# A layer whose expert weights stream through a ring of SBUF slots: 12 slots in place of 9, paid for by moving the front buffers into the late slots

## The reference

```python
def moe_ffn(x2, w_router, b_router, w_gu, b_gu, w_down, b_down):
    logits = (x2 @ w_router + b_router).astype(jnp.float32)
    top_vals, top_idx = lax.top_k(logits, TOP_K)                  # 4 of 32
    gates = jax.nn.softmax(top_vals, axis=-1).astype(x2.dtype)
...
        h = x2[tok] @ w_gu[e] + b_gu[e]                           # 1024 x 2048 for each expert
        g = jnp.minimum(h[:, :D_FF], SWIGLU_LIMIT)
        u = jnp.clip(h[:, D_FF:], -SWIGLU_LIMIT, SWIGLU_LIMIT)
        y = (u + 1.0) * (g * jax.nn.sigmoid(SWIGLU_ALPHA * g))
        return y @ w_down[e] + b_down[e]                          # 1024 x 1024 for each expert
```

## Time and profile before

| | |
|---|---|
| median of 3 runs | 1331.33 us (1329.54 to 1331.73) |
| profiled execution, device time | 1332.64 us |
| its span, first to last instruction | 1330.8 us |
| PE busy | 1113.0 us, 84% |
| DVE, ACT, POOL busy | 359.2, 157.1, 24.3 us |
| read from HBM | 443.69 MB, 334 GB/s over the span |
| mean granted TensorE clock | 0.939 |

### The profile page before, as it was taken

One profiled execution on the slowest core, in us unless ns is written; L12 is line 12 of the kernel. 1 busy time (PEld: TensorE's weight loads), 2 busy tenths in 40 slices (PEclk: granted clock), 3 DMA queues, 4 the chain that ended last, 5 costly groups with the idle time before them and its releaser, 6 DMA issues.

```text
span 1330.8 us, 19889 instructions
## 1 busy us (share of the span) xinstructions
PE 1113.0 (84%) x7904; PEld 463.9 (35%) x7905; DVE 359.2 (27%) x1183; ACT 157.1 (12%) x360; POOL 24.3 (2%) x26
## 2 busy tenths in 40 slices
PE   4999999999998665768956799797986987989895
PEld 3758845845332111112311133232321322323231
DVE  1513521124232121112211133231222322323224
ACT  0020300211111000001100011110110110111111
POOL 6000000000000000000000000000000000000000
PEclk9999999996999888789988799998998997999998
DMA  9933346305999999999899957999899899897980
GB/s 313 318 123 131 131 168 269 127 12 221 413 419 427 426 428 425 426 427 385 360 427 425 426 253 322 426 426 425 335 426 426 331 427 426 334 429 330 427 374 32
DMA packets 57460, 445.04 MB, mean 334 GB/s; under 512 B 4784, under 2 KB 7872, under 8 KB 24192
## 3 DMA queue, kind: packets, MB, share of 16 engines
q1 hardware_dynamic: 55888, 438.35, 79.9%
q0 software_dynamic: 976, 5.26, 1.2%
q10 hardware_dynamic: 576, 1.14, 0.3%
HBM read 443.69 MB, written 1.05 MB: 334 GB/s over the span
## 4 chain that ended last, share of the span: by engine, by line
PE 53%; DMA 41%; DVE 3%; SPq 2%; issue 1%; ACT 0%; DVEq 0%
DMA ring<-in_w_down 32%; PE bank L728 16%; PE bank L759 8%; DMA ring<-in_w_gu 8%; PE bank L425 6%; PE bank L440 6%; PE bank L685 4%; PE bank L616 2%; PE bank L672 2%; SPq L319 2%; DMA ring<-in_xT 1%; PE bank L678 1%; PE bank L738 1%; PE bank L723 1%; PE bank L604 1%
## 5 line engine op out<-in xcount | busy, mean ns | idle before, releaser
L728 PE MATMUL bank<-ring,memT_sb 128*32 128x512 f32 x3264 | 418.9, 658 | 138.9 <-DMA ring<-in_w_gu 138.9
L728 PEld LDWEIGHTS bank<-ring,memT_sb 128*32 128x32 f32 x3264 | 105.0, 116 | 423.9 <-issue 211.9
L1249 DVE TENSOR_SCALAR memK<-bank 128x256 f32<-128x256 f32 x51 | 21.7, 425 | 660.8 <-PE bank L728 660.8
L759 PE MATMUL bank<-ring,memV 128*32 128x512 f32 x1632 | 196.1, 598 | 0.2 <-DMA ring<-in_w_down 0.2
L685 PE MATMUL bank<-memV,memK 64*128 64x512 f32 x416 | 106.1, 629 | 0.7 <-ACT memV L921 0.7
L913 ACT ACTIVATE memK<-memK 128x256 f32<-128x256 f32 x51 | 21.2, 417 | 554.6 <-DVE memK L1249 554.6
L759 PEld LDWEIGHTS bank<-ring,memV 128*32 128x32 f32 x1632 | 47.9, 109 | 76.5 <-issue 61.1
L425 PE MATMUL bank<-ring 128*128 128x256 f32 x320 | 72.6, 390 | 0.8 <-issue 0.8
L425 PEld LDWEIGHTS bank<-ring 128*128 128x128 f32 x320 | 62.4, 196 | 9.9 <-issue 1.0
L685 PEld LDWEIGHTS bank<-memV,memK 64*128 64x128 f32 x416 | 37.2, 193 | 78.3 <-issue 76.7
L672 PE MATMUL bank<-res,memT_sb 128*32 128x256 f32 x832 | 56.5, 390 | 0.0
(11 more groups left out here) (250 smaller groups left out, 753.2 us busy)
## 6 DMA issues: line engine op xcount, KB each, us to landing
ring<-in_w_gu SPq DMA_DIRECT2D x128, 2048.0 KB, 31.9
ring<-in_w_down SPq DMA_DIRECT2D x64, 2048.0 KB, 27.0
ring<-in_w_in SPq DMA_DIRECT2D x5, 2048.0 KB, 21.1
ring<-in_w_ck SPq DMA_DIRECT2D x2, 2048.0 KB, 12.3
ring<-in_w_out SPq DMA_DIRECT2D x2, 2048.0 KB, 7.9
ring<-in_w_cv SPq DMA_DIRECT2D x2, 2048.0 KB, 8.2
ring<-in_w_cq SPq DMA_DIRECT2D x2, 2048.0 KB, 8.5
ring<-in_w_co SPq DMA_DIRECT2D x2, 2048.0 KB, 7.9
```

Source lines behind the costliest of these rows:

```text
L728: ins = mm(hidden(g), xg[:, kk, c, :], gate_and_up(w[:, kk, :], g), start=False, stop=2 * c + kk == KT - 1, skip_group_check=True)
L759: ins = mm(strip(7, 2 * d + b), actT[:, b, 2 * c + gg, :], wd[:, gg, b, 512 * d:512 * d + 512], start=c == 0 and gg == 0, stop=c == 1 and ...
```

## The change

- `RING` is 12 and `UNROLL` is 2. The ring then holds two experts. It is 192 KB of each partition.
- Slots 8 to 11 exist in full, and in the front they hold what had buffers of their own: `memV` and `ebuf` in slot 8, `memK` and `memT_sb` in slot 9, `qbuf` and the tables (`early_c`) in slot 10, `xk`/`tT` and `lnp` in slot 11; `akT` and `akrot` lie in slot 7. The small buffers of the experts' passes are in one tensor `wk`.
- The first twelve pieces wait: slots 6 and 7 for `mixer_done`; 4, 5, 0, 1 for their front pieces; slot 10 for the last score matmul of the cross-attention (`cs_ready`, L587 before), slot 9 for its last transpose (`cpT_ready`, L594), slot 8 for unit `oT1` (L604), slots 2 and 3 for `co_t1` (L616), slot 11 for unit `logit` (L633).
- POOL issues no load. ACT issues its loads at the start behind the tables, the first layer norm's parameters and `b_down` with them. The second norm's parameters are issued by ACT when the first norm is done. The third's are issued by SP into slot 6 when the last pass of expert 30 has used its first piece.
- The values are computed once for each row (two groups of eight matmuls in place of four), and ACT copies them to the four windows in five copies in place of one. The 64 columns of zeros are gone.
- `mark_gates` multiplies in place (`eq` for `gq`) and waits for `hot_ready`; `act` is written over `ucl`. The memset of `ysb` stands behind the router's last reduction, and that of `scatT` behind `sums_open`.

```diff
-UNROLL = 3
+UNROLL = 2
-RING = 9
+RING = 12
-RING_ORDER = [6, 7, 4, 5, 0, 1, 2, 3, 8]
+RING_ORDER = [6, 7, 4, 5, 0, 1, 10, 9, 8, 2, 3, 11]
...
-                    elif s < RING - 1:
+                    elif s < 8:
                         sp.wait_ge(mixer_done, 1)
+                    elif s == 8:
+                        wait_unit(sp, "oT1")
+                    elif s == 9:
+                        sp.wait_ge(cpT_ready, MEM_H)
+                    elif s == 10:
+                        sp.wait_ge(cs_ready, MEM_H)
                     else:
-                        sp.wait_ge(sums_open, 1)
-                else:
-                    if n == RING:
-                        sp.wait_ge(tables_ready, 1)
-                    pe_, pc_ = divmod(n - RING, EXP_CHUNKS)
-
-                    sp.wait_ge(chunk_used[pc_], sp.value_load(cum_i[0:1, pe_:pe_ + 1], min_val=1, max_val=MAX_PASSES))
+                        wait_unit(sp, "logit")
                 load_chunk(e, c, n)
...
+            sp.wait_ge(tables_ready, 1)
             with sp.Fori(1, LOOPS) as it:
                 load_later(it * UNROLL, UNROLL * EXP_CHUNKS)
-            load_later(LOOPS * UNROLL, (N_EXP % UNROLL) * EXP_CHUNKS)
+
+            sp.wait_ge(chunk_used[0], sp.value_load(cum_i[0:1, N_EXP - UNROLL:N_EXP - UNROLL + 1], min_val=1, max_val=MAX_PASSES))
+            sp.dma_start(ln3p, ln_p[2:3].to_broadcast([P, 2 * D])).then_inc(ln_landed[2], 16)
...
-            for c in range(NCHUNK):
+            for t in range(TT):
                 for k in range(KT):
-                    ins = mm(b1[:, c * P:(c + 1) * P], xT_pad[:, k, c * CHUNK:c * CHUNK + P], w[:, k, P:2 * P], start=k == 0, stop=k == KT - 1)
+                    ins = mm(b1[:, t * P:(t + 1) * P], xk[:, k, t * P:(t + 1) * P], w[:, k, P:2 * P], start=k == 0, stop=k == KT - 1)
...
+            act_e.wait_ge(zero_done, 1)
+            for i in range(3):
+                act_e.dma_start(bgu_raw[N_EXP * i:N_EXP * (i + 1), :], b_gu).then_inc(bgu_landed, 16)
+            act_e.dma_start(res[:], x.rearrange("(t p) n -> p t n", p=P)).then_inc(x_landed, 16)
+            act_e.dma_start(router_w[:], w_router.rearrange("(k p) n -> p k n", p=P)).then_inc(router_landed, 16)
+            act_e.dma_start(brow[:], b_router.rearrange("(o n) -> o n", o=1).to_broadcast([P, N_EXP])).then_inc(router_landed, 16)
+            act_e.dma_start(lnp, ln_p[0:1].to_broadcast([P, 2 * D])).then_inc(ln_landed[0], 16)
+            act_e.dma_start(bdown, b_down).then_inc(bdown_landed, 16)
...
+            vals = unit_banks("akav")[1][:, 0:2 * P].rearrange("p (t d) -> p t d", t=TT)
+            af(av[:, 1, :], vals[:, 0, :], ACT.Copy)
+            af(av[:, 3, :], vals[:, 1, :], ACT.Copy)
+            af(av[CHUNK:P, 0, :], vals[0:CHUNK, 0, :], ACT.Copy)
+            af(av[0:CHUNK, 2, :], vals[CHUNK:P, 0, :], ACT.Copy)
+            af(av[CHUNK:P, 2, :], vals[0:CHUNK, 1, :], ACT.Copy).then_inc(taken["akav"], 1)
```

More of the change, by code:

```diff
@@ L81, in sem @@
             return ctx.enter_context(nc.semaphore(name))
[L84 to L88, removed]
-        res = sb("res", [P, TT, D])
[L90 to L96, removed]
+        ring = sb("ring", [P, RING * SLOT])
+        res = sb("res", [P, TT, D])
         late_c = sb("late_c", [P, L_W])
@@ L109, in slot_words @@
             return ring[:, i * SLOT:(i + 1) * SLOT]
-        xT_pad = xT_sb.rearrange("p (k t) -> p k t", k=KT)
-        xk = xT_pad[:, :, CHUNK:]
-        tT = xT_sb[:, 0:KT * SEQ].rearrange("p (k t) -> p k t", k=KT)
+        half = SLOT // 2
+        S6, S7, S8, S9, S10, S11 = (slot_words(i) for i in range(6, 12))
+        memV = S8[:, 0:half].rearrange("p (t n) -> p t n", t=2)
+        ebuf = S8[:, half:SLOT]
+        memK = S9[:, 0:half].rearrange("p (k t) -> p k t", k=KT)
+        memT_sb = S9[:, half:SLOT].rearrange("p (k t) -> p k t", k=KT)
+        qbuf = S10[:, 0:half]
+        early_c = S10[:, half:half + E_W]
+        xk = S11[:, 0:half].rearrange("p (k t) -> p k t", k=KT)
+        tT = xk
+        lnp = S11[:, half:SLOT]
+        ln3p = S6[:, 0:2 * D]
         aqT = qbuf[:, 0:1024].rearrange("p (m t) -> p m t", m=4)
@@ L173, in layer_program @@
[L173 to L188, removed]
+        bgu_raw = S9[:, 0:half]
+        bgu_rest = S8[:, 0:half]
+        xg = wk[:, 0:256].rearrange("p (b g s) -> p b g s", b=2, g=GROUPS)
+        xrows = wk[:, 256:256 + Q]
+        eq = wk[:, 512:768].rearrange("p (t k s) -> p t k s", t=TT, k=TOP_K)
+        hot = wk[:, 768:832].rearrange("p (t s) -> p t s", t=TT)
@@ new lines, in layer_program @@
+        hotg1 = wk[:, 832:896].rearrange("p (t s) -> p t s", t=TT)
+        hotg = wk[:, 896:1152].rearrange("p (t f s) -> p t f s", t=TT, f=GROUPS)
+        gcl = wk[:, 1152:1152 + Q]
+        ucl = wk[:, 1408:1408 + Q]
+        act = ucl
+        sgm = wk[:, 1664:1664 + Q]
+        actT = wk[:, 1920:1920 + 2 * P].rearrange("p (b g s) -> p b g s", b=2, g=GROUPS)
+        bdown = wk[0:N_EXP, 1152:1152 + D]
+        ysb = wk[:, 2176:2688]
+        onehot = wk[:, 2176:2432].rearrange("p (j e) -> p j e", j=8)
@@ new lines, in layer_program @@
+        tmp8 = wk[:, 2432:2688].rearrange("p (j e) -> p j e", j=8)
+        scatT = wk[:, 2688:2944]
+        gT = wk[0:N_EXP, 2688:2688 + SEQ].rearrange("p (t n) -> p t n", t=TT)
+        rel = wk[:, 2944:2952]
+        gate = wk[:, 2952:2960]
+        first, last = wk[:, 2960:2961], wk[:, 2961:2962]
+        began = wk[:, 2962:2963]
+        osel = wk[:, 2963:2964].bitcast(BF16)[:, 0:1]
+        npass = wk[:, 2964:2965]
+        steps = wk[:, 2968:2976]
+        npass_i = wk[:, 2976:3008].bitcast(I32)
@@ L367, in link @@
                 pool.wait_ge(pool_step, steps_done[0])
-            nc.gpsimd.memset(xT_pad[:, :, 0:CHUNK], 0.0)
+            nc.gpsimd.memset(av[0:CHUNK, 0, :], 0.0)
             nc.gpsimd.memset(akT[:, 0:CHUNK], 0.0)
@@ L389, in _ @@
             nc.gpsimd.tensor_copy(bgu3[low, :], bgu_raw[low, :]).then_inc(bgu_split, 1)
[L391 to L395, removed]
-                if i == 1:
-                    wait_unit(pool, "oT1")
-                    nc.gpsimd.dma_start(bdown, b_down).then_inc(bdown_landed, 16)
         @block.tensor
@@ L822, in _ @@
             wait_unit(act_e, "akav")
-            af(av, unit_banks("akav")[1][:].rearrange("p (c d) -> p c d", c=NCHUNK), ACT.Copy).then_inc(taken["akav"], 1)
+            vals = unit_banks("akav")[1][:, 0:2 * P].rearrange("p (t d) -> p t d", t=TT)
[4 more added lines that the diff above has]
+            af(av[CHUNK:P, 2, :], vals[0:CHUNK, 1, :], ACT.Copy).then_inc(taken["akav"], 1)
             def take_T(u, dst, which=(0, 1)):
@@ L1147, in _ @@
             take_transposed("x2T1", 1)
-            v.memset(ysb, 0.0).then_inc(y_ready, 1)
-            v.memset(scatT, 0.0).then_inc(scT_ready, 1)
             dve.wait_ge(router_landed, 32)
@@ L1202, in _ @@
             link(v.reduce_sum(rel, tmp8, AX_X))
+            v.memset(ysb, 0.0).then_inc(y_ready, 1)
             eqf = eq.rearrange("p t k s -> p (t k) s")
-            gqf = gq.rearrange("p t k s -> p (t k) s")
             def mark_tokens(chain):
@@ L1229, in _ @@
             mark_tokens(link)
-            mark_gates(link)
+            mark_gates(link, 1)
             dve.wait_ge(gT_read, 1)
+            dve.wait_ge(sums_open, 1)
+            v.memset(scatT, 0.0).then_inc(scT_ready, 1)
             v.memset(nwt[:, 14:15], 0.0).then_inc(aT_ready, 1)
@@ L1256, in _ @@
                 dve.wait_ge(scT_done, j + 1)
-                mark_gates(chain)
+                mark_gates(chain, j + 2)
                 assert count[0] == STEPS
```

87 lines of the change are left out of this document (35 added, 52 removed).

## The result

The changed kernel takes 1260.1 us in the median (1256.36 to 1261.69, four runs) against 1331.53 (1329.54 to 1333.35, four runs) for the kernel before. The ratio is 0.946, its 95% interval 0.9435 to 0.9485. The forecast was 1264 (1255 to 1275). The profiled execution took 1260.32 us with a span of 1258.5, where the sum said 1263.5: the sum is 5.0 us too long.

The account below looks back on a forecast made before the run. PE paces the front, transfers and PE in turn the experts, with transfers as the floor. 1330.8 - 53.1 - 14.7 + 1.0 - 3.6 (values) + 3.1 = 1263.5 us of span, so 1264.0, range 1255 to 1275.

Parts of the forecast that it names:

- The ring: Experts' part: twelve slots remove transfer stops at five experts and shorten the one at expert 15; -53.1 us.
- The start's 14.7: End of the front: three additional pieces issued early leave 180 in the stream behind it, not 183; -14.7 us.
- The recurrence: Expert stream: a piece lands 4.91 us behind the last or some 8 behind issue; issues wait for the release `RING` back.
- +1.0: Expert 1's second pass: piece 18 waits for its first use there and lands late, a gap of 1.0 us.
- The small loads: Kernel start: norm parameters and `b_down` join the loads and come ahead of `xT`, delaying it by 3.1 us.
- That stays: Kernel end: the 65.1 us from the landing of expert 30's last piece to the end, bound by PE, are unchanged.
- hardly 1 us before the piece: Kernel end: after the change PE reaches the wait for expert 30's last piece hardly 1 us before it lands.
- The start goes badly: Rival, chance 0.09: ACT's load issues block at the start and PE waits, 5 to 7 us more, 1270.
- Three pieces ahead, and no more: Rival, chance 0.04: SP can't have more in flight, so other dips replace those in the experts' part; 1317.
- Slower: Rival, chance 0.04: the expert stream itself slows, a piece taking 5.43 us; 1358.

Follow-up runs that it names:

- e1: Changed kernel with each expert piece waiting for the release nine pieces back, not twelve, at the start too; 1328.0 us, ratio 0.9957 to the kernel before.
- e2: Changed kernel with nine pieces ahead at the start and twelve later; 1275.6 us, ratio 0.9579 to the kernel before.
- e3: Changed kernel with twelve pieces ahead at the start and nine later; 1324.9 us, ratio 0.9945 to the kernel before.
- e5: Changed kernel with a look-ahead of eleven pieces throughout; 1268.3 us, ratio 0.953 to the kernel before.
- e6: Changed kernel with a look-ahead of ten pieces throughout; 1294.2 us, ratio 0.9715 to the kernel before.
- e8: Changed kernel with the loads of the first norm's parameters and `b_down` issued behind ACT's first two activations; 1261.3 us, ratio 0.9472 to the kernel before.
- e4: Changed kernel with `xT` ahead of all small loads but the gate parameters; 1250.7 us, ratio 0.9382 to the kernel before.

## Why the prediction was right, and by how much each step

**The ring, right.** From the first pass to expert 30's last piece the steps gave 53.1 + 14.7 - 1.0 = 66.8 us less; it is 66.6. The five dips are gone, the one at expert 15 is 7.8 us where about 7 were forecast, transfers stand idle from 315 to 327 where 320 to 332 was forecast, and e1 brings the six dips and the time back by moving one wait. A pass stayed at 14.6 us.

**The start's 14.7, right in size, wrong as a separate term.** It needs the twelve slots later on: 15.5 us with them (e2), 3.1 without (e3). The recurrence that I had carried through the passes holds this. Over the span with twelve it gave 9.8 us for e5, 32.2 for e6, 13.7 for e2 and 66.6 for e1 and e3; measured are 11.8, 35.5, 15.7, 68.0 and 66.8. My sum for the case at hand came out right because it removed both together. The **+1.0** for piece 18 is not borne out: its issue came 29.7 us behind the first release (357.23 - 327.49) and not 30.9, and from 350 to 365 the rate is 420 GB/s on average, a loss of 0.3 us.

**The small loads, mis-sized.** The step "I take +3.1 us on `xT`, the end where all of it comes ahead" is the one that failed. `xT` landed at 19.8, 0.8 us later than before. At the values' start the shift was 97.19 - 96.57 = 0.6 us in place of 3.1: 2.5 of the 5.0 us. That busy engines make `xT` a matter of what moves beside it was sound (with other loads out of the way it lands 7.8 or 10.8 us earlier). But the step took all the bytes of the two loads to move ahead of `xT`. They were issued only at 13.7 and 14.1, since ACT had been held, they landed 9.4 and 10.4 us behind it, and e8 shows no cost. The Trainium skill's page "DMA: Bandwidth & Descriptors", section "Issuing engines are not separate DMA queues", stays right here: loads that ACT issues slow the one that SP issues, by 10.8 us in e4.

**The rest of the 5.0.** Between the values and the first pass the changed kernel gained another 1.2 us, 0.9 of them in the cross-attention. The chains, before and after:

```profile
259.83 2.77 PE bank L594 x12
262.60 7.35 PE bank L604 x32
```

```profile
258.49 0.66 PE bank L575 x4
259.15 6.91 PE bank L585 x32
```

Before, the granted clock was 0.50 from 260 to 262, its lower level of 1.2 GHz; after, it is 1.00 through the whole stretch:

```profile
250.00:272.00 22.00, 19.78 (x83) 14.03 (x83) 5.70 (x15) 8.64 (x24) 0.00 (x0) 1.00 0.90 352
```

The edits don't account for this fall. From the start of the scores (`cs_ready`) to the matmuls behind this group it is 19.6 us before and 18.7 after, and of the nine experiments, none of which edits this stretch, two have 18.7 again and seven 19.5 to 19.9; e5 shows 2.77 and 7.35 us once more. So these 0.9 us were luck: the profiled execution of the changed kernel is one of the three without the fall. Why the clock falls there in the others, no run shows. The other 0.3 are four short matmuls of the router's end, in windows with a clock of 0.76 before and 0.84 after.

At the end "That stays" gave 65.1 us from expert 30's last piece; it is 1258.5 - 1194.9 = 63.6. Before, PE had stood waiting for this piece and the three ahead of it, 7.9 us in all, and began again at a granted clock of 0.83. The window of the kernel before from the landing on:

```profile
1265.00:1275.00 10.00, 9.26 (x73) 2.98 (x77) 0.00 (x0) 0.98 (x2) 0.00 (x0) 0.83 1.02 433
```

Its first 16 matmuls on the down pieces took 2.92 us where the same ones take 1.85 in the chain above, and the bias matmuls 0.43 in place of 0.22, and the 64 of the next pass 7.29 in place of 6.87. That is 1.07 + 0.21 + 0.42 = 1.7 us; 0.2 of it goes again into a wait for expert 31's last piece, which is new. After, PE waits only 0.55 us for expert 30's piece, as forecast ("hardly 1 us before the piece"), and its clock is 1.00 behind it. With the ring's 66.6 in place of 66.8 the account is 2.5 + 1.2 + 1.5 - 0.2 = 5.0.

**The rivals.** *The start goes badly* had its mechanism: ACT's issues do block, 7.6 us in one of them. But they were over at 16.6 us, not 45, and ACT, which loaded a table then, stood idle for 12.2 us ahead of its first computation at 30.1; PE did not wait for it. *Three pieces ahead, and no more* falls by the windows and by e1 to e3. Its premise was wrong as well, as the issues of `w_gu` from 400 us on show:

```profile
DMA to landing us min/median/max: 7.7/36.4/47.2
```

With twelve slots the longest time from issue to landing is 47.2 us, 9.6 pieces, where it was 42.0, 8.5 pieces, with nine. *Slower*: the rate is 423 to 427 GB/s in the windows with three more pieces ahead.

## What to carry to other kernels

Where consumers of a ring are uneven, look at the one that holds its pieces longest. Compare the time until its first release with the free slots at that moment times the time of a piece. A slot that still shortens this gap is worth a part of a stall for each such consumer, and one beyond it little (here 33.8, 25.9 and 8.2 us). A lead at the start lasts only if the ring behind it is as deep. And see what else is in flight beside the load that the first matmul waits for: here it was 10.8 us of its landing, more than some of the planned edits brought. Before a difference of a microsecond is put down to an edit, look at the same stretch in runs that don't touch it.

## What the runs showed of the hardware

- An issue of a transfer can hold its engine. SP stood up to some 12 us at one issue in the experts' part, as the chain of the changed kernel shows from 495.96 on (12.12 us), while the rate stayed at 427 GB/s; that cost nothing. ACT's load of 16 KB was held for 7.6 us behind ACT's nine loads of the start. It cost nothing here either, as ACT then waited 12.2 us for its first computation, but it put off the two loads behind it.
- The granted clock was lower in stretches where PE stood waiting: 0.83 behind the waits for expert 30 before, and after the change 0.85 over the one-pass experts (PE busy for 106 of 160 us), 0.92 from 620 to 770 (117 of 150), 0.99 from 790 to 1220 (397 of 430) and 1.00 in the two windows in which PE was busy throughout. Without the waits at expert 30 the matmuls behind them took 1.7 us less. It was low elsewhere too: 0.50 from 315 to 327, with PE busy for 10.6 of 12 us.
- The clock can differ between profiled executions in a stretch that no edit touches: in the cross-attention of the changed kernel it was 1.00, in e5 0.57 from 258 to 262, and the stretch took 18.7 us in three of the ten executions with this code and 19.5 to 19.9 in the other seven.
